# Three groups of small TensorE products placed one or two weight slots later in a two-layer encoder kernel

## The reference, cut to what matters

```python
z = h @ w_in                                  # h = rms_norm(x)
a, gate, q, k, v = jnp.split(z, [s1, s2, s3, s4], axis=-1)
u = a * jax.nn.sigmoid(gate)
u = causal_depthwise_conv(u, dw_w) + dw_b     # 31 taps, 1024 channels
u = jax.nn.silu(layer_norm(u, ln_g, ln_b))
q = rms_norm(q.reshape(b, t, N_Q_HEADS, HEAD_DIM), qn_g)      # 16 heads of 64
k = rms_norm(k.reshape(b, t, N_KV_HEADS, HEAD_DIM), kn_g)     # 2 heads of 64
v = v.reshape(b, t, N_KV_HEADS, HEAD_DIM)
o = banded_sink_attention(q, k, v, sinks)     # window of 2 chunks of 64
return jnp.concatenate([u, o], axis=-1) @ w_out
```

## Time and profile before

| | us |
|---|---|
| median of three runs (2100.74, 2103.23, 2107.02) | 2103.23 |
| the profiled execution's own time | 2106.77 |
| span of the profiled execution, first to last instruction | 2105.0 |
| TensorE busy in it | 2075.5 (99%) |
| VectorE busy | 1358.3 (65%) |
| ScalarE busy | 1099.4 (52%) |
| GpSimd busy | 556.6 (26%) |

### The profile page before, as it was taken

How to read it: one execution, slowest core, us unless ns; L and a number is a source line. 1 busy time by engine, 2 the same in 40 slices (tenths; PEclk the granted TensorE clock), 3 DMA queues, 4 the chain that set the end, 5 groups by cost and what they waited for, 6 DMA issues and landing times.

```text
span 2105.0 us, 24328 instructions
## 1 busy us (share of the span) xinstructions
PE 2075.5 (99%) x9634; PEld 1728.1 (82%) x9634; DVE 1358.3 (65%) x1378; ACT 1099.4 (52%) x1260; POOL 556.6 (26%) x292
## 2 busy tenths in 40 slices
PE   9998999999999999999999999999999999999999
PEld 8888777888888888888888888888888888888887
DVE  5787868954888358873442333478738994389832
ACT  6677555644555445554544444555545554455542
POOL 3676630023000420004454444310040003400033
PEclk9999999999999999999999999999999999999999
DMA  7533355556555565645566565556466555655554
GB/s 251 161 120 120 131 178 192 180 169 230 180 202 180 193 206 193 236 159 181 180 199 191 183 187 190 171 201 243 155 213 219 177 183 190 236 184 188 188 190 161
DMA packets 208577, 394.29 MB, mean 187 GB/s; under 512 B 11472, under 2 KB 22096, under 8 KB 208464
## 3 DMA queue, kind: packets, MB, share of 16 engines
q1 hardware_dynamic: 207888, 392.21, 55.7%
q10 hardware_dynamic: 576, 0.53, 0.1%
HBM read 390.60 MB, written 2.10 MB: 187 GB/s over the span
## 4 chain that ended last, share of the span: by engine, by line
PE 90%; issue 3%; DVE 3%; ACT 2%; POOL 1%; DMA 0%; SPq 0%; DVEq 0%; ACTq 0%; POOLq 0%
PE pair L654 14%; PE pair L656 14%; PE pair L655 14%; PE pair L731 9%; PE pair L729 9%; PE pair L730 9%; PE pair L714 5%; PE pair L715 5%; PE pair L716 5%; PE tbank L744 2%; DVE w_lo L1595 1%; DVE pair L1748 1%; POOL cv L620 1%; ACT w_hi L1161 1%; DVE s_raw L1990 0%
## 5 line engine op out<-in xcount | busy, mean ns | idle before, releaser
L1161 ACT ACTIVATE w_hi<-w_raw 128x1024 fp32r<-128x1024 f32 x608 | 642.3, 1059 | 653.5 <-PE pair L656 418.9
L608 POOL TENSOR_TENSOR w_lo<-w_raw,w_hi 128x1024 fp32r<-128x1024 f32 x191 | 472.3, 2473 | 1533.1 <-ACT w_hi L1161 1533.1
L1595 DVE TENSOR_TENSOR w_lo<-w_raw,w_hi 128x1024 fp32r<-128x1024 f32 x417 | 537.6, 1290 | 490.8 <-ACT w_hi L1161 490.6
L729 PE MATMUL pair<-w_hi,xT_hi 128*128 128x512 f32 x880 | 342.4, 389 | 0.4 <-DVE w_lo L1595 0.4
L731 PE MATMUL pair<-w_hi,xT_lo 128*128 128x512 f32 x880 | 342.4, 389 | 0.0
L730 PE MATMUL pair<-w_lo,xT_hi 128*128 128x512 f32 x880 | 342.3, 389 | 0.0
L1161 ACT ACTIVATE w_hi<-s_raw 128x1536 fp32r<-128x1536 f32 x154 | 229.2, 1488 | 160.0 <-PE pair L731 119.1
L1595 DVE TENSOR_TENSOR w_lo<-s_raw,w_hi 128x1536 fp32r<-128x1536 f32 x154 | 269.7, 1761 | 59.5 <-ACT w_hi L1161 59.2
L654 PE MATMUL pair<-w_hi,yT_hi 128*128 128x512 f32 x704 | 274.7, 390 | 0.0
L656 PE MATMUL pair<-w_hi,yT_lo 128*128 128x512 f32 x704 | 274.0, 389 | 0.0
L655 PE MATMUL pair<-w_lo,yT_hi 128*128 128x512 f32 x704 | 273.9, 389 | 0.0
(11 more groups left out here) (187 smaller groups left out, 2659.7 us busy)
## 6 DMA issues: line engine op xcount, KB each, us to landing
w_raw<-in_w_down SPq DMA_DIRECT2D x176, 512.0 KB, 4.2
w_raw<-in_w_up SPq DMA_DIRECT2D x110, 512.0 KB, 6.5
w_raw<-in_w_gate SPq DMA_DIRECT2D x110, 512.0 KB, 3.6
w_raw<-in_sc_in SPq DMA_DIRECT2D x96, 512.0 KB, 3.9
s_raw<-in_w_gate SPq DMA_DIRECT2D x44, 768.0 KB, 8.6
s_raw<-in_w_up SPq DMA_DIRECT2D x44, 768.0 KB, 8.2
w_raw<-in_w_in SPq DMA_DIRECT2D x52, 512.0 KB, 4.0
w_raw<-in_w_out SPq DMA_DIRECT2D x32, 512.0 KB, 3.5
```

What stands on the lines that cost most here:

```text
L608: nc.gpsimd.tensor_tensor(w_lo[at], raw(o), w_hi[at].bitcast(F32), ALU.subtract).then_inc(w_lo_pool, 1)
L729: nc.tensor.matmul(b, x_hi(k, t), w_hi[:, r, kk, :], start=(first[t] and kk == 0), stop=False)
L1161: nc.scalar.activation(w_hi[:, o % RING, tiles_of(o), :], raw(o), ACT.Copy).then_inc(w_hi_ready, 1)
L1595: nc.vector.tensor_tensor(w_lo[at], raw(o), w_hi[at].bitcast(F32), ALU.subtract).then_inc(w_lo_dve, 1)
```

## The change

TensorE's list is altered in these places. The transposes of the keys come after slot 27 and no longer after slot 25. The query transposes of the first eight heads and both pairs of score products of `hh` 0 come one slot later (after slots 33, 34 and 35); the first score products of `hh` 1 stay behind slot 35. The first value products come after slot 40 and no longer after slot 39, so that the probability transposes of `hh` 1 follow them with no slot between. The second value products of `hh` 1 and the query transposes of the second eight heads come after slot 43 and no longer after slot 42. Nothing else is altered.

```diff
             narrow("kv", 2, SN)
-            slots("q0", 0, 6, x_hi, x_lo, last=SD)
+            slots("q0", 0, SD, x_hi, x_lo)
 
             pe.wait_ge(qk_normed, 1)
             transposes("kT", [k_twice[:, t, g, :, :].rearrange("p w d -> p (w d)")
                               for g in range(HKV) for t in range(TT)])
-            slots("q0", 6, SD, x_hi, x_lo)
-            slots("q1", 0, 5, x_hi, x_lo, last=SD)
+            slots("q1", 0, 6, x_hi, x_lo, last=SD)
             query_transposes(0)
-            slots("q1", 5, 6, x_hi, x_lo, last=SD)
+            slots("q1", 6, 7, x_hi, x_lo, last=SD)
             score_products(0, 0, 2)
-            slots("q1", 6, 7, x_hi, x_lo, last=SD)
+            slots("q1", 7, SD, x_hi, x_lo)
             score_products(0, 2, 4)
-            slots("q1", 7, SD, x_hi, x_lo)
             score_products(1, 0, 2)
...
             prob_transposes(0, 0, 2)
-            late(3, 4)
+            late(3, 5)
             value_products(0, 0, 2)
-            late(4, 5)
             prob_transposes(1, 0, 2)
             late(5, 6)
             value_products(1, 0, 2)
             prob_transposes(1, 2, 4)
-            late(6, 7)
+            late(6, 8)
             value_products(1, 2, 4)
             query_transposes(1)
-            late(7, 8)
             score_products(2, 0, 2)
```

## The result

| | before | changed |
|---|---|---|
| median of 6 runs each, side by side (us) | 2101.97 | 2114.11 |
| lowest and highest | 2099.95, 2107.02 | 2111.34, 2118.15 |
| ratio of the times, 95% interval | | 1.0056 [1.0040, 1.0072] |
| profiled execution's own time, span | 2106.77, 2105.0 | 2111.42, 2109.6 |

The forecast was 2107.8 with a range up to 2112.5: the direction was right, the size two and a half times too small. Yet the profiled execution took 2111.42, and 2111.4 was forecast for it. So what failed lies between one execution and the median. The hit is partly luck: the twelve runs of the changed kernel in this document took 2110.26 to 2118.15, and only four of them 2111.42 or less.

A forecast was written before the change was run, and what follows sets the result against it. TensorE was taken as the bound (90% of the chain). New pauses and uncovered work, 9.3 us, less removed pauses and slow clock, 4.5, gave 4.6 by the marks; on the median 2103.23 that is 2107.8, range 2100.5 to 2112.5.

The forecast's parts named there:

- The step that failed: From profiled execution to median: 2106.77 lay 3.5 above the median, so 4.6 was added to 2103.23, giving 2107.8.
- the one clock term of the sum: Score products of hh 0: the pause of 1.78 goes, and 1.6 us of slow clock behind it is saved.
- the last mark: Second products of hh 2: TensorE 4.6 us late there, carried unchanged to the end.
- Keys: Key transposes: first pause joins the second, 0.6 us uncovered, kT copy 9 later; pauses 1.4, 0.7, 0.6 for slots 29, 31, 33.
- Scores of hh 0: Score products of hh 0: score_rows starts at 123.6, 5.0 later; pause of 1.78 gone; TensorE 0.6 us late afterwards.
- the two prices: DVE's w_lo of slot 36: 2.45 us beside POOL at work, or 1.23; the prediction took 2.45.
- Scores of hh 1: Second score products of hh 1: new pause of about 2.0 us for the banks, ending at 131.0 to 131.3.
- Values: Value products of hh 1: pause of 0.91 removed; that of 1.30 at 150.56 stays at 1.5.
- Scores of hh 2: Second products of hh 2: score_rows at 169.6 instead of 164.30, TensorE waits 1.9 us for that bank.
- The rival of slow clock: Clock falls after pauses at 99.4, 129.6 and 168.2, adding 5 us less what later waits absorb: 2111.5; chance 0.25.
- hidden copy: Rival at the keys: w_lo of slot 29 ready by 99.4 despite ACT's later copy, 3.9 us gained, 2099.3; chance 0.12.
- absorbed delay: Rival at the stage's end: DVE's convolution taps set it, so 4.6 shrinks to under 1.5 us, 2104; chance 0.13.

The follow-up runs named there:

- the keys alone: Kernel before with only the transposes of the keys moved to after slot 27: median 2107.5 us, ratio 1.0026 to the kernel before.
- slot 43 alone: Kernel before with only slot 43 put ahead of the last value products of hh 1 and the query transposes: 2110.3 us, ratio 1.0036.
- all but the keys: Changed kernel with the transposes of the keys back after slot 25: median 2109.5 us, ratio 1.0029 to the kernel before.
- ACT's copies later: Changed kernel with ACT's copy to kT two w_hi later and each copy to qT one w_hi later: 2108.4 us, ratio 1.0016 to before.
- ACT and DVE re-ordered: Changed kernel, ACT's copies later, DVE's w_lo of slot 26 ahead of key norms, convolution taps later, division early: 2108.1 us, ratio 1.0018 to before.
- the two with the division early: DVE's division heads_out(1) ahead of its w_lo of slot 46, in slot 43 alone (2104.7 us, 1.0005) and in the changed kernel (2110.0, 1.0032).

## Why the prediction was wrong

**The step that failed** is this one: "that one lies 3.5 above the median, so on the median 2107.8". It took the 3.5 for an offset that both kernels have. It was slow clock of that one execution: another profile of before took 2103.08 with nearly the same waits, and the stretches at 220 to 228 and 256 to 260 at full clock; it lost 3.4 us less to the clock. With it failed the one clock term of the sum, 1.6 us given back. The clock gave 1.7 back in the first pair of profiles. Over all runs it didn't: the changed kernel lost 3 us to it in the mean. So the right sum for the median was 2102 to 2104, plus 7, plus 3.

The rest of the sum, its waits and added work, came to 6.2, and the two first profiles less their slow clock stand 6.3 apart. This agreement is in part luck. At the last mark, the second products of `hh` 2, the same two profiles stand 6.5 apart (165.40 and 171.88), and up to there the changed kernel had lost 1.7 less to the clock: 8.2 at equal clock, 2.0 more than the sum. The work behind that mark took 1.9 of it back (0.8 in the second pair of profiles), where the prediction carried the delay to the end unchanged.

**Keys.** Right in mechanism and nearly in size. The removed pause joined the other (3.51 against 1.84 + 1.01), the copy to `kT` held back slot 29 (1.32; forecast 1.4). The pauses for 31 and 33 were 0.37 and 0.35 instead of 0.7 and 0.6. The transposes came at 94.62, 1.4 earlier than said, since this profile has no slow clock behind the pause of 3.51; the kernel with the keys alone has it, .50 at 88 to 92. Why the same pause brings it in one case and not in the other is open.

**Scores of hh 0.** `score_rows` started at 121.93, not 123.6: the `w_lo` of slot 36 took 1.78, between the two prices. So TensorE was not 0.6 late at the first products of hh 1 but 0.8 early (123.89 against 124.70). This error was in the kernel's favour.

**Scores of hh 1.** The pause was 2.19 (forecast 2.0), at 130.57 instead of 131.0 to 131.6.

**Values.** The pause of 0.91 went, that of 1.30 shrank to 0.71 (forecast 1.5).

**Scores of hh 2.** The mis-sized term. "Waits 1.9 for that bank" measured 3.61, since the small addition on DVE met POOL's `w_lo` and `score_rows` came at 171.26, not 169.6. Moving the division out of that place took 4.2 us off the changed kernel and 5.6 off slot 43 alone; 1 to 2 us of each are the order, the rest came with a higher clock.

**The rival of slow clock** had 0.25 and 2111.5. It names what took the time out of the range, but not quite as it was told. Of its three falls two are there in both profiles of the changed kernel, behind the pauses at 130.57 and 171.88. In the second profile:

```profile
128.00:132.00 4.00, 1.79 (x9) 1.36 (x8) 3.38 (x10) 3.97 (x18) 0.00 (x0) 0.92 0.48 131
132.00:136.00 4.00, 4.00 (x23) 3.58 (x22) 3.54 (x5) 4.00 (x7) 2.22 (x1) 0.65 0.00 2
172.00:176.00 4.00, 3.79 (x22) 3.52 (x21) 2.67 (x8) 1.67 (x3) 0.03 (x1) 0.57 0.13 45
```

The third, behind the pause at 99.31, is not, and the falls of before at 88 to 96 and 120 to 124 are gone, so up to 200 us the count is even, two falls in each kernel. The rival did not see the next place. The first value products of `hh` 3 wait 2.5 us in all four profiles (at 199.59 and 199.56 before, 206.88 and 206.59 changed), and behind that same pause the clock is low for longer in the changed kernel. Stretches of the second profile of before, then of the second of the changed kernel:

```profile
200.00:204.00 4.00, 4.00 (x26) 3.71 (x26) 3.02 (x5) 3.29 (x6) 3.71 (x4) 0.73 0.38 119
204.00:208.00 4.00, 3.76 (x19) 2.87 (x18) 2.82 (x7) 1.57 (x4) 3.86 (x4) 0.85 0.39 143
```

```profile
204.00:208.00 4.00, 1.46 (x8) 1.44 (x7) 2.02 (x6) 4.00 (x8) 3.71 (x3) 0.81 0.16 63
208.00:212.00 4.00, 4.00 (x20) 4.00 (x20) 3.82 (x7) 1.27 (x3) 3.57 (x5) 0.50 0.59 188
212.00:216.00 4.00, 4.00 (x20) 3.28 (x19) 1.92 (x5) 2.46 (x5) 2.67 (x2) 0.84 0.20 74
```

The clock of 0.50 is the lower of its two levels, 1.2 GHz. Between 196 and 216 us both profiles of before lose 1.7 us to the clock and both of the changed kernel 3.4. The profiles of the keys alone, all but the keys, slot 43 alone, ACT's copies later and ACT and DVE re-ordered lose 3.4 there too, the two with the division early 1.7. If other executions do as these, it is about half of the 3 us; that isn't shown. That the clock of the changed kernel is lower in most other runs is measured; which stretches make it so there is open, since only these two executions have a profile. The hidden copy is refuted (the copy delays POOL, and moving it takes the waits away), and of the absorbed delay, which needed 3 us, only 1.9 and 0.8 were there: at equal clock 8.2 and 8.0 us at the second products of hh 2 (165.36 and 171.61 in the second profiles, with 1.7 of clock), 6.3 and 7.2 at the end.

## What to carry to other kernels

Work out a change as a sum of waits and work at one clock, and set it against the median only after more than one profile of the kernel before: here two profiles of one kernel differed by 3.7 us, 3.4 of it slow clock, almost as much as the whole forecast. Before moving a product to a later slot on TensorE, read which copy follows it on ACT and what is queued behind that copy; if the copy moves along, most of the cost goes (here 6.7 us at equal clock became 1.8, with three copies moved), but one must look anew for what then waits. In a queue shifted by some microseconds, look at each small two-input instruction on DVE for a long one on POOL that it may now start behind.

## What the runs showed that I had not expected

- An addition of 128 x 8 on DVE took 0.16, 0.50 and 2.25 us in three orders of the same work; the last ended within 0.02 us of POOL's `w_lo`.
- The time of single runs of an unchanged kernel follows the granted clock: 2100.7 in the mean at .997 (25 runs), 2108.5 at .993 (13 runs). This spread of 8 us is larger than the effect that I had forecast.
- A 128 x 128 float32 matmul on ones is two records and 0.23 us for both (6.41 us for 28), at full clock.
- A kernel with fewer and shorter waits (ACT and DVE re-ordered) had the lowest clock of all, .9930. A lower clock thus didn't come from longer waits alone; what brings it there stays open.
